# Moving the recurrent layer's head norm into its state-update stage in a hybrid decoder step

## The reference, cut to what matters

```
def _rmsnorm(x, g):
    x32 = x.astype(jnp.float32)
    y = x32 * lax.rsqrt(jnp.mean(x32 * x32, axis=-1, keepdims=True) + NORM_EPS)
    return (y * g.astype(jnp.float32)).astype(x.dtype)

def _hgrn2(h, s0, lb, w_in, g_norm, w_out):
    ...
    o, s_new = _gla_scan(q, k, v, log_f, s0)
    o = _rmsnorm(o, g_norm) * jax.nn.silu(g.astype(jnp.float32))
    return o.reshape(b, t, wv).astype(h.dtype) @ w_out, s_new.astype(h.dtype)
```

## Time and profile before

| What | us |
|---|---|
| Median of 3 runs | 2593.35 (2593.27 to 2594.52) |
| The profiled execution | 2586.57 |
| Its span in the trace | 2584.8 |
| PE busy | 2437.6 (94%) |
| DVE busy | 1319.1 (51%) |
| ACT busy | 734.7 (28%) |
| POOL busy | 16.4 (1%) |
| Mean granted clock of PE, as a share of 2.4 GHz | 0.939 |

### The profile page before, as it was taken

One profiled execution on the slowest core, in us unless ns is written; L12 is line 12 of the kernel. 1 busy time (PEld: TensorE's weight loads), 2 busy tenths in 40 slices (PEclk: granted clock), 3 DMA queues, 4 the chain that ended last, 5 costly groups with the idle time before them and its releaser, 6 DMA issues. The chain is left out here.

```text
span 2584.8 us, 45650 instructions
## 1 busy us (share of the span) xinstructions
PE 2437.6 (94%) x19270; PEld 2065.8 (80%) x19270; DVE 1319.1 (51%) x2358; ACT 734.7 (28%) x1767; POOL 16.4 (1%) x18
## 2 busy tenths in 40 slices
PE   8989988899999888999999899999999998989998
PEld 6668865699986756999888766899985787648998
DVE  2267374356542473665443285356541865525665
ACT  2134372221012333210232194221021445522200
POOL 0000000000000000000000010000000000000000
PEclk8999799999999978999999867999999997889999
DMA  9997607767733325677343255567662865293440
GB/s 347 305 248 172 202 29 241 281 229 269 254 128 133 98 74 195 229 259 263 132 141 132 68 147 167 192 232 276 243 173 71 179 182 157 64 316 111 170 175 31
DMA packets 287345, 472.74 MB, mean 183 GB/s; under 512 B 14956, under 2 KB 105149, under 8 KB 286662
## 3 DMA queue, kind: packets, MB, share of 16 engines
q1 hardware_dynamic: 272370, 456.04, 54.3%
q10 hardware_dynamic: 14770, 13.76, 1.7%
HBM read 448.72 MB, written 38.04 MB: 188 GB/s over the span
## 5 line engine op out<-in xcount | busy, mean ns | idle before, releaser
L598 PE MATMUL PS<-hT,ring 128*128 128x132 f32 x2048 | 250.3, 277 | 6.1 <-DVE hT L723 4.2
L598 PEld LDWEIGHTS PS<-hT,ring 128*128 128x128 f32 x2048 | 238.3, 190 | 12.6 <-issue 11.8
L598 PE MATMUL PS<-mT,arena 128*128 128x132 f32 x1536 | 185.3, 276 | 0.0
L598 PEld LDWEIGHTS PS<-mT,arena 128*128 128x128 f32 x1536 | 179.1, 190 | 0.0
L2628 PE MATMUL PS<-hT,ring 128*128 128x264 f32 x768 | 172.7, 386 | 0.3 <-DVE hT L480 0.3
L2628 PEld LDWEIGHTS PS<-hT,ring 128*128 128x128 f32 x768 | 145.1, 190 | 25.1 <-issue 0.6
L735 DVE TENSOR_TENSOR arena<-arena,PS 128x264 f32<-128x264 f32 x224 | 89.7, 427 | 129.4 <-PE PS L598 128.2
L682 ACT ACTIVATE arena<-arena 128x528 f32<-128x528 f32 x64 | 41.1, 643 | 312.1 <-DVE arena L735 312.1
L1443 DVE COPY arena<-PS 64x512 f32<-64x512 f32 (+1 forms) x160 | 94.2, 589 | 66.2 <-PE PS L1317 65.1
L598 PE MATMUL PS<-arena,ring 128*128 128x132 f32 x1024 | 127.5, 278 | 0.0
L598 PE MATMUL PS<-mT,ring 128*128 128x132 f32 x1024 | 125.7, 276 | 0.0
(11 more groups left out here) (479 smaller groups left out, 4408.6 us busy)
## 6 DMA issues: line engine op xcount, KB each, us to landing
arena<-in_w_ada SPq DMA_DIRECT2D x36, 2048.0 KB, 12.1
ring<-in_w_mlp_in SPq DMA_DIRECT2D x32, 2048.0 KB, 8.6
ring<-in_w_mlp_out SPq DMA_DIRECT2D x32, 2048.0 KB, 8.5
ring<-in_w_ada SPq DMA_DIRECT2D x12, 2048.0 KB, 19.1
ring<-in_ssd_w_in SPq DMA_DIRECT2D x12, 2048.0 KB, 7.9
ring<-in_nsa_w_in SPq DMA_DIRECT2D x10, 2048.0 KB, 9.1
arena<-in_cache_nsa_kv SPq DMA_DIRECT2D x64, 256.0 KB, 10.3
ring<-in_cache_nsa_kv SPq DMA_DIRECT2D x64, 256.0 KB, 7.8
```

The lines of the kernel that those rows point to most:

```text
L598: ins = nc.tensor.matmul(PS[:, bank, at:at + HALF], lhs[:, k, p * 128:(p + 1) * 128], rhs[:, k, :], start=opens and k == 0, stop=closes an ...
```

## The change

The closing block of the recurrent layer goes. Its work for the prompt is done in the state-update block, in four pairs of heads. ACT multiplies the gate by the gain and squares the pairs ahead of everything else that it has there, loads the function table and takes the roots of a pair when PE has summed it. POOL, which had nothing in this block, multiplies each pair by its gate and then by its root. PE's sums stand behind rounds 4, 6, 8 and 10, in PSUM bank 6, so that the rounds now take turns in six banks instead of seven. From the second pair on a sum also waits for the roots of the pair before it, since both use the same bank. The samples' share follows at the end: DVE squares it, PE sums, ACT takes the root, and DVE multiplies. SP's wait for the stores moves to the head of the next block (`first`). Nothing in the diff touches the state-space layer.

```diff
@@ -2416,6 +2416,13 @@
                 P = Place(after_A - 2048 - 1024 - 2048)
                 k_tok = P(2, D)
                 s_p = P(HG_H, 128)
+                P = Place(after_A + 2048)
+                rs = P(HG_H, SEQ)
+                own = mT_flat[:, HG_H * SEQ:HG_H * T]
+
+                def two_heads(v, p):
+                    return v[:, 2 * p:2 * p + 2, 0:SEQ]
+
                 with nc.Block() as block:
                     @block.sync
                     def _(sp):
@@ -2426,11 +2433,9 @@
                                 stored.on(sp.dma_start(hg_p[0, 0].rearrange("h k v -> k h v"), s_p), 16)
                             sp.wait_ge(given.sem, given.at(h + 1))
                             stored2.on(sp.dma_start(dst[:, h], S[h]), 16)
-                        sp.wait_ge(stored2.sem, stored2.at(128))
-                        sp.wait_ge(stored.sem, stored.at(16))
 
                     rounds = [(r, x, 4 * r + c) for r in range(2) for x in range(2) for c in range(4)]
-                    bank = lambda i: (2, 3, 4, 5, 6, 0, 1)[i % 7]
+                    bank = lambda i: (2, 3, 4, 5, 0, 1)[i % 6]
 
                     @block.scalar
                     def _(act):
@@ -2441,12 +2446,36 @@
                         for c in range(4):
                             aux_taken.on(nc.scalar.activation(kt[32 * c:32 * c + NB], PS[0:NB, 4:6, c * 128:(c + 1) * 128],
                                                               ACT.Copy))
+                        step = stepper(act, act_step)
+                        nc.scalar.activation(g, g, ACT.Copy, scale=hg_gain)
+                        for p in range(4):
+                            prompt_squared.on(nc.scalar.activation(two_heads(rs, p), two_heads(hT, p), ACT.Square))
+                        load_norm_table()
+                        for p in range(4):
+                            act.wait_ge(group_summed.sem, group_summed.at(p + 1))
+                            y = two_heads(rs, p)
+                            step(nc.scalar.activation(y, PS[:, 6, :].rearrange("p (h n) -> p h n", h=2), ACT.Ln,
+                                                      bias=eps[:, :], scale=1.0 / 128))
+                            roots.on(nc.scalar.activation(y, y, ACT.Exp, scale=-0.5))
                         for r in range(2):
                             act.wait_ge(out_ready.sem, out_ready.at(r + 1))
                             for c in range(4):
                                 ins = nc.scalar.activation(o_tok[:, 4 * r + c, :],
                                                            PS[32 * c:32 * c + NB, 7, r * 128:(r + 1) * 128], ACT.Copy)
                             out_taken.on(ins)
+                        act.wait_ge(group_summed.sem, group_summed.at(5))
+                        step(nc.scalar.activation(own, PS[:, 6, 0:HG_H * NB], ACT.Ln, bias=eps[:, :], scale=1.0 / 128))
+                        roots.on(nc.scalar.activation(own, own, ACT.Exp, scale=-0.5))
+
+                    @block.gpsimd
+                    def _(gp):
+                        for p in range(4):
+                            x = two_heads(hT, p)
+                            gp.wait_ge(prompt_squared.sem, prompt_squared.at(p + 1))
+                            pool_step.on(nc.gpsimd.tensor_tensor(x, x, two_heads(g, p), ALU.mult))
+                            gp.wait_ge(pool_step.sem, pool_step.at(p + 1))
+                            gp.wait_ge(roots.sem, roots.at(p + 1))
+                            nc.gpsimd.tensor_tensor(x, x, two_heads(rs, p), ALU.mult)
 
                     @block.tensor
                     def _(pe):
@@ -2481,13 +2510,22 @@
                         pe.wait_ge(aux_taken.sem, aux_taken.at(4))
                         pe.wait_ge(aux_made.sem, aux_made.at(1))
                         for i, (r, x, h) in enumerate(rounds):
-                            if i == 5:
+                            if i == 4:
                                 pe.wait_ge(mm_taken.sem, mm_taken.at(6))
-                            if i >= 7:
-                                pe.wait_ge(pt_taken.sem, pt_taken.at(i - 6))
+                            if i >= 6:
+                                pe.wait_ge(pt_taken.sem, pt_taken.at(i - 5))
                             c = h % 4
                             pt_ready.on(nc.tensor.matmul(PS[:, bank(i), :], kt[32 * c:32 * c + NB, r, :],
                                                          vm[32 * c:32 * c + NB, r, 4 * x:4 * x + 4, :], start=True, stop=True))
+                            if i in (4, 6, 8, 10):
+                                p = i // 2 - 2
+                                pe.wait_ge(prompt_squared.sem, prompt_squared.at(p + 1))
+                                if p:
+                                    pe.wait_ge(roots.sem, roots.at(p))
+                                for y in range(2):
+                                    ins = nc.tensor.matmul(PS[:, 6, y * SEQ:(y + 1) * SEQ], ones[:, 0:128], rs[:, 2 * p + y, :],
+                                                           start=True, stop=True)
+                                group_summed.on(ins)
                             if i == 14:
                                 read_out(0)
                         pe.wait_ge(out_taken.sem, out_taken.at(1))
@@ -2496,6 +2534,9 @@
                         for h in range(HG_H):
                             ins = nc.tensor.transpose(PS[:, 7, h * NB:(h + 1) * NB], o_tok[:, h, :], ident[0:NB, 0:NB])
                         pv_ready.on(ins)
+                        pe.wait_ge(roots.sem, roots.at(4))
+                        pe.wait_ge(last_gated.sem, last_gated.at(1))
+                        group_summed.on(nc.tensor.matmul(PS[:, 6, 0:HG_H * NB], ones[:, 0:128], own, start=True, stop=True))
 
                     @block.vector
                     def _(v):
@@ -2521,40 +2562,22 @@
                                 v.sem_inc(given.sem, 1)
                                 given.given += 1
                         v.wait_ge(pv_ready.sem, pv_ready.at(1))
-                        step(nc.vector.tensor_copy(hT[:, :, SEQ:T], PS[:, 7, 0:64].rearrange("p (h b) -> p h b", h=HG_H)))
+                        xs, y = hT[:, :, SEQ:T], own.rearrange("p (h b) -> p h b", h=HG_H)
+                        step(nc.vector.tensor_copy(xs, PS[:, 7, 0:64].rearrange("p (h b) -> p h b", h=HG_H)))
+                        last_gated.on(nc.vector.tensor_tensor(y, xs, xs, ALU.mult))
+                        v.wait_ge(last_gated.sem, last_gated.at(1))
+                        v.wait_ge(prompt_squared.sem, prompt_squared.at(4))
+                        step(nc.vector.tensor_tensor(xs, xs, g[:, :, SEQ:T], ALU.mult))
+                        v.wait_ge(roots.sem, roots.at(5))
+                        nc.vector.tensor_tensor(xs, xs, y, ALU.mult)
+                states_out, prompt_out = stored2.at(128), stored.at(16)
                 end_stage()
 
-
-                with nc.Block() as block:
-                    @block.scalar
-                    def _(act):
-                        for h in range(HG_H):
-                            given.on(nc.scalar.activation(mT[:, h, :], hT[:, h, :], ACT.Square))
-                        for h in range(HG_H):
-                            act.wait_ge(mm_ready.sem, mm_ready.at(h + 1))
-                            act_step.on(nc.scalar.activation(mT[:, h, :], PS[:, h, 0:T], ACT.Ln, bias=eps[:, :],
-                                                             scale=1.0 / 128))
-                        act.wait_ge(act_step.sem, act_step.at(HG_H))
-                        for h in range(HG_H):
-                            exp_ready.on(nc.scalar.activation(mT[:, h, :], mT[:, h, :], ACT.Exp, scale=-0.5))
-
-                    @block.tensor
-                    def _(pe):
-                        for h in range(HG_H):
-                            pe.wait_ge(given.sem, given.at(h + 1))
-                            mm_ready.on(nc.tensor.matmul(PS[:, h, 0:T], ones[:, 0:128], mT[:, h, :], start=True, stop=True))
-
-                    @block.vector
-                    def _(v):
-                        step = stepper(v, dve_step)
-                        step(nc.vector.tensor_scalar_mul(g, g, hg_gain))
-                        for h in range(HG_H):
-                            v.wait_ge(given.sem, given.at(h + 1))
-                            step(nc.vector.tensor_tensor(hT[:, h, :], hT[:, h, :], g[:, h, :], ALU.mult))
-                            v.wait_ge(exp_ready.sem, exp_ready.at(h + 1))
-                            step(nc.vector.tensor_tensor(hT[:, h, :], hT[:, h, :], mT[:, h, :], ALU.mult))
-                end_stage()
-                return hT, 1
+                def first(sp):
+                    sp.wait_ge(stored2.sem, states_out)
+                    sp.wait_ge(stored.sem, prompt_out)
+
+                return hT, 1, first
             return parts, rest
 
         dt_raw = signal("dt_raw")
```

## The result

| | before | the change |
|---|---|---|
| Median of 6 runs each, us | 2593.66 (2587.59 to 2598.26) | 2577.88 (2575.11 to 2584.91) |
| The profiled execution, us | 2586.57 | 2579.96 |
| Its span, us | 2584.8 | 2578.2 |
| Mean granted clock of PE | 0.939 | 0.943 |

The ratio is 0.9949 with a 95% interval of 0.9934 to 0.9965: 9 to 17 us less, 13 in the middle. The change is faster by 0.5%, which is small but clear of the spread.

A forecast was written before the change was run, and what follows sets the result against it. PE bounds the kernel on average, but the closing stage is a chain of single steps and DVE bounds the state update. Removing the stage, -14.85, plus late rounds, +2.5, gives -12.35: 2593.35 to 2581.0 us, range 2573 to 2587.

The forecast's parts named there:

- The likeliest case: Whole program: closing stage removed, rounds late, -12.35 us, giving 2581.0 us; chance 0.50 for a gain of 10 to 14.
- The removed stage and the new end: Closing stage: 17.12 us go, the samples' share and the engines' meeting take 2.27 us, so 14.85 us less.
- The work under the rounds: State-update block: ACT's gate, squares, table load and roots and POOL's eight products, 10.2 us, are hidden under DVE's rounds.
- The late rounds: State-update block: sums waiting for roots hold up PE's rounds behind them, so the rounds end about 2.5 us later.
- I let the clock fall where it did: State-update block: PE's clock assumed to fall from 2.4 to 1.2 GHz at about 943 us, as in the profile before.
- the 1.6 us: State-update block: a pair of sums on PE at the lower clock, taken as 2/8 of 6.27 us.
- rival A: State-update block: the clock stays high and no round is late; gain 14.85, or 16.6 with a faster last read-out; chance 0.30.
- The loss of the bank: State-update block: round 14 waits for DVE's ninth round, not its eighth; alone this brings round 15 some 0.6 us late.
- Rival B: State-update block: no two rounds run side by side, rounds end 17 us later, a loss of 2 us overall; chance 0.03.
- Rivals C and D: State-update block: POOL doubles DVE's instruction times, 18.3 us more (C, 0.03); POOL's products stop DVE, 10.2 us (D or mixtures, 0.14).
- Rival E: State-space layer: already joined before, so only one closing stage goes and no second 17 us; a two-stage gain given no chance.
- Against the median: Whole program: the local sum of -12.35 us applied to the earlier runs' median, 2593.35, gives 2581.0 us.

The follow-up runs named there:

- the early sums: The change with sums behind rounds 4, 5, 6, 8 in two banks and the read-out of heads 0 to 3 behind round 15: stretch 31.00 us.
- six banks and no POOL: The kernel before with six PSUM banks for the rounds instead of seven, nothing else: stretch 42.48 us, against 41.72 before.
- the spaced sums: The change with sums 1 to 3 behind rounds 4, 6, 10 in bank 7, seven round banks, round 15 before the read-out, sum 4 after: 24.65, 24.64 us.
- spare matmuls: The spaced sums plus one spare matmul during ACT's read-out copies and two behind the samples' sum: stretch 25.07 us, median 2567.61 beside 2566.62 without.
- the fourth sum moved: The change with its fourth sum alone moved behind round 15 and ACT's roots for it behind the first copies: stretch 27.40 us.

## Why the prediction was right, and where it wasn't

The likeliest case was forecast at -12.35 us, and the first profile's stretch gave -12.33. That agreement is better than the reasons deserve, so point by point:

- **The removed stage and the new end** (-14.85 forecast). Measured 2.34 us in the place of 17.12, forecast 2.27: -14.78. Within it the samples' chain took 2.05 us, where I had 1.75, and the meeting of the engines 0.29, where I had 0.52. Right as a whole, by two errors that cancel.
- **The work under the rounds.** ACT's gate by gain took 2.06, its squares 2.17 together, the roots 1.35 a pair; POOL's eight products 1.27 each and over at 963.9. Counted from the start of the stretch, ACT's roots ended at 13.4 us and POOL at 14.8, where I had named 15.4 and 16.4 as the latest. All hidden, and the runs with twice POOL's work and with none show it for POOL. SP's wait: nothing, as forecast.
- **The late rounds** (+2.5 forecast). Measured +2.46 in the first trace, with the idle times ahead of rounds 11 and 15, as written. That is luck, for two errors cancel. A pair of sums takes 2.0 us at the lower clock, not 1.6: the 6.27 us that the 1.6 was taken from ran at 0.50 only until about 970.2 and at 1.00 behind it. With that and the clock falling where I let it fall, the term is 3.8 us, as the runs with doubled POOL and without POOL show. But in the first trace the clock fell later, 5.2 us into the stretch instead of 3.4, and that took it back to 2.46. The term is not a property of the code: it was 2.46 once and 0.5 in the other three executions, since in those the clock held until 10.8 us into the stretch. "I let the clock fall where it did" and the 1.6 us are the steps that failed. The likelier gain in the stretch is about 14.25, near rival A's 14.85, and I had given that case 0.30. The measured median difference of 15.8 us, or 13 by the ratio, can't tell the two apart.
- **The reason for the late rounds** was half right. I had written that a sum that waits for roots holds up the rounds. In the change's first trace PE waits for roots for 0.47 and 0.30 us, with an early fall of the clock not at all once it is down, and the early sums, without such waits, are no better. A pair of sums and one set of rounds cost PE 4.0 us together at 1.2 GHz, however many rounds are in the set, and two are too few. The loss of the bank (0.6 forecast, 0.87 measured alone) was nearly right.
- **Rival B** (rounds one at a time): fallen, eight passes take as long as two. **Rivals C and D** (POOL against DVE): fallen. 60 updates took 17.01 and 17.00 us beside POOL in the repeats of the change, and 17.00 with six banks and no POOL. The Trainium skill (SBUF — State Buffer, Who interferes with whom) allows that for a DVE instruction with at most one input in SBUF. These runs agree, and show that the decay factor taken per partition doesn't count as a second. **Rival E**: only one stage went, as read.
- **Against the median.** The profiled executions lay 6.6 us apart and the medians 15.8. Carrying a local sum over to the median came out within the spread here, and no better than that: the same comparison, made three times, gave 15.8, 13.6 and 19.7 us. The difference of the two profiled spans would have been the wrong number to judge by, since 9.5 us against the change arose ahead of the stretch.

## What to carry to other kernels

When full matmuls are put between thin ones that run side by side, count how many of the thin ones stand between two full ones, and what the consumer takes for them: a set costs PE the same whether it holds one or four. Do the sum at the lower clock too, because in all thirteen executions here the stretch ended up there. And judge a change of a few microseconds by a stretch that starts and ends at the same instructions, over several executions, never by one pair of spans.

## What the runs showed of the hardware that was not expected

- The granted clock falls at different points of the same code: 2.7 to 10.9 us into this stretch over thirteen executions. The same kernel's stretch is 27.45 or 29.39 us accordingly. The Trainium skill (TensorE: Matmul & The Clock Gate, Part 1) says that the gate isn't tied to the kernel's start; the trace agrees.
- In all three executions with the spaced sums (one of them with spare matmuls), the clock came back ahead of the last read-out (1.93 instead of 3.60 us). In the change it didn't, and with the fourth sum moved it was back for 3.4 us and fell again as that read-out began. What brings it back is open: it is not the missing idle time of PE alone, since the early sums kept PE without a gap for 23 us and had the lower clock from 957.9 to 981.7.
- One, two or four rounds of 8 rows for different quarters of the array took 2.07, 2.08 and 2.09 us at 1.2 GHz, and a set of rounds or a pair of full sums 2.0 us from one start to the next.
